# Gate and up of a feed-forward block: four of eight chunk pairs by seven products instead of three

## What is computed

```
y = _rms(h, norm_ffn_g[i])
h = h + (jax.nn.silu(y @ w_gate[i]) * (y @ w_up[i])) @ w_down[i]
```

## Time and profile before

| | |
|---|---|
| median of 3 runs | 1391.5 us (1391.1 to 1393.21) |
| the profiled execution: its time / its span | 1391.67 / 1389.9 us |
| PE busy | 1383.6 us (100%), 6233 matmuls |
| DVE busy | 1123.0 us (81%) |
| ACT busy | 822.8 us (59%) |
| POOL busy | 109.6 us (8%) |
| HBM read and written | 295.14 and 26.26 MB |
| clock granted to PE | full (2.4 GHz) in all 40 slices |

### The profile page before, as it was taken

How to read it: one execution, slowest core, us unless ns; L and a number is a source line. 1 busy time by engine, 2 the same in 40 slices (tenths; PEclk the granted TensorE clock), 3 DMA queues, 4 the chain that set the end, 5 groups by cost and what they waited for, 6 DMA issues and landing times.

```text
span 1389.9 us, 16815 instructions
## 1 busy us (share of the span) xinstructions
PE 1383.6 (100%) x6233; PEld 1133.3 (82%) x6233; DVE 1123.0 (81%) x1338; ACT 822.8 (59%) x1111; POOL 109.6 (8%) x96
## 2 busy tenths in 40 slices
...
GB/s 333 247 209 211 200 178 230 285 242 227 277 260 264 210 172 269 258 274 232 280 241 198 257 227 240 275 307 244 277 245 289 209 265 260 256 269 299 191 204 151
DMA packets 178538, 339.30 MB, mean 244 GB/s; under 512 B 12593, under 2 KB 36397, under 8 KB 178328
## 3 DMA queue, kind: packets, MB, share of 16 engines
q1 hardware_dynamic: 158968, 289.56, 64.0%
q0 software_dynamic: 6400, 23.49, 7.7%
...
HBM read 295.14 MB, written 26.26 MB: 231 GB/s over the span
## 4 chain that ended last, share of the span: by engine, by line
PE 92%; DMA 3%; DVE 3%; SPq 1%; ACT 1%; issue 0%; ACTq 0%; DVEq 0%
PE acc L2174 14%; PE acc L2177 14%; PE acc L2176 14%; PE acc L1996 14%; PE acc L1997 13%; PE acc L1998 13%; PE sp L2174 1%; PE sp L2177 1%; PE sp L2176 1%; PE tp L2177 1%; PE tp L2174 1%; PE tp L2176 1%; DVE w_lo L1278 1%; DMA w_raw<-in_w_in 1%; PE sp L2285 1%; DMA parked<-tile 1%
## 5 line engine op out<-in xcount | busy, mean ns | idle before, releaser
L868 ACT ACTIVATE w_hi<-w_raw 128x1024 fp32r<-128x1024 f32 x479 | 500.4, 1057 | 367.3 <-PE acc L1998 208.8
L1278 DVE TENSOR_TENSOR w_lo<-w_raw,w_hi 128x1024 fp32r<-128x1024 f32 x468 | 567.1, 1226 | 170.1 <-ACT w_hi L868 164.6
L1996 PE MATMUL acc<-w_lo,hh 128*128 128x512 f32 x528 | 207.9, 394 | 0.0
L1998 PE MATMUL acc<-w_hi,hl 128*128 128x512 f32 x528 | 205.6, 389 | 0.0
L1997 PE MATMUL acc<-w_hi,hh 128*128 128x512 f32 x528 | 205.6, 389 | 0.0
L2174 PE MATMUL acc<-w_lo,yh 128*128 128x512 f32 x512 | 199.3, 389 | 0.6 <-DVE w_lo L1278 0.6
L2177 PE MATMUL acc<-w_hi,yl 128*128 128x512 f32 x512 | 199.2, 389 | 0.0
L2176 PE MATMUL acc<-w_hi,yh 128*128 128x512 f32 x512 | 199.2, 389 | 0.0
L1996 PE MATMUL acc<-w_lo,yh 128*128 128x512 f32 x352 | 137.6, 391 | 0.3 <-DVE w_lo L1278 0.3
L1997 PE MATMUL acc<-w_hi,yh 128*128 128x512 f32 x352 | 137.0, 389 | 0.0
L1998 PE MATMUL acc<-w_hi,yl 128*128 128x512 f32 x352 | 137.0, 389 | 0.0
...
## 6 DMA issues: line engine op xcount, KB each, us to landing
...
```

The source lines that it names most:

```text
L868: act.activation(w_hi[:, v % SPL], src, ACT.Copy).then_inc(hi_ready, 1)
L1278: dve.tensor_tensor(w_lo[:, v % SPL], src, w_hi[:, v % SPL].bitcast(F32), ALU.subtract).then_inc(lo_ready, 1)
L1996: pe.matmul(dst, xh[:, f, tk], w_lo[:, v % SPL, k], start=(f == 0), stop=False)
L1998: last = pe.matmul(dst, xl[:, f, tk], w_hi[:, v % SPL, k], start=False, stop=(f == CK * n - 1))
```

## The change

`PAIR_PLAN` gets a fourth quad in place of a plain chunk pair (chunk 3) and a new order: 4 quads and 8 plain chunks, 24 splits. The first two quads' "g" now stand at the head of the pair, and the last four splits are the plain up chunks 7, 4, 5, 6. `TRIPLES` goes from 3 to 4, so that the sums of activations take 16 KB per partition, and the places of all other work in the pair are given anew. In the first pair one up chunk moves behind the gate's last two. To make room, `h_wide` now lies over the last quarter of `hh` for its first two uses and in `tile[7]` for the third, `h_sums` to where `big` lies, and one scratch result of ACT's squares to `big`.

```
-PAIR_PLAN = plain(0, 4, 3) + quad("g", 0) + plain(1, 4) + quad("g", 1) + quad("g", 2) + quad("u", 0) + quad("t", 0)
-PAIR_PLAN += quad("s", 0) + plain(1, 5) + quad("u", 1) + plain(0, 6, 5) + quad("t", 1) + quad("s", 1) + quad("u", 2)
-PAIR_PLAN += quad("t", 2) + quad("s", 2) + plain(0, 7) + plain(1, 7, 3, 6)
+PAIR_PLAN = quad("g", 0) + quad("g", 1) + plain(0, 4, 6) + quad("u", 0) + quad("t", 0) + quad("s", 0)
+PAIR_PLAN += quad("g", 2) + quad("u", 1) + quad("t", 1) + quad("s", 1) + quad("g", 3) + quad("u", 2)
+PAIR_PLAN += quad("u", 3) + plain(0, 7, 5) + quad("t", 2) + quad("s", 2) + quad("t", 3) + quad("s", 3)
+PAIR_PLAN += plain(1, 7, 4, 5, 6)
-SUMS = dict(copied={1: [0], 5: [1], 10: [2]}, summed={0: 5, 1: 11, 2: 14})
+SUMS = dict(copied={0: [0], 2: [1], 9: [2], 12: [3]}, summed={0: 3, 1: 5, 2: 14, 3: 16})
-FIRST_PLAN += quad("s", 1) + plain(1, 5) + plain(0, 6, 7) + plain(1, 6, 7)
+FIRST_PLAN += quad("s", 1) + plain(0, 6, 7) + plain(1, 5, 6, 7)
-           1: dict(hidden=1, turn=2, m1=12, mix=19, gate=20, low=21, silu=21, put=9, fetch=12, **SUMS),
-           2: dict(hidden=1, sums=4, turn=5, m1=12, mix=19, gate=20, low=21, silu=21, put=10, fetch=13, **SUMS),
+           1: dict(hidden=2, turn=11, low=22, put=12, fetch=13, m1=17, mix=21, gate=21, silu=23, **SUMS),
+           2: dict(sums=4, hidden=2, turn=11, low=22, put=12, fetch=13, m1=17, mix=21, gate=21, silu=23, **SUMS),
...
-TRIPLES, PAIRS_OF_DOWN = 3, 2
+TRIPLES, PAIRS_OF_DOWN = 4, 2
...
+        with ExitStack() as first:
+            first.enter_context(nc.sbuf_tensor("hh_front", [P, 12, S], F32))
+            h_wide_front = first.enter_context(nc.sbuf_tensor("h_wide", [P, PAIRS_OF_DOWN, 4, P], F32))
```

More of the change, by code:

```diff
@@ L120 @@
               + plain(1, 7, 4, 2) + plain(0, 6) + plain(1, 6, 3)]
-SUMS = dict(copied={1: [0], 5: [1], 10: [2]}, summed={0: 5, 1: 11, 2: 14})
 FIRST_PLAN = plain(0, 2) + plain(1, 2) + plain(0, 3) + plain(1, 3) + quad("g", 0) + quad("g", 1) + quad("u", 0)
 FIRST_PLAN += plain(0, 4) + quad("t", 0) + quad("s", 0) + plain(1, 4) + quad("u", 1) + plain(0, 5) + quad("t", 1)
-FIRST_PLAN += quad("s", 1) + plain(1, 5) + plain(0, 6, 7) + plain(1, 6, 7)
-FIRST_AT = dict(resid=1, turned=2, low2=3, request=3, low3=11, m1=13, mix=18, gate=19, silu=19,
+FIRST_PLAN += quad("s", 1) + plain(0, 6, 7) + plain(1, 5, 6, 7)
+FIRST_AT = dict(resid=1, turned=2, low2=3, request=3, low3=10, m1=13, mix=18, gate=19, silu=19,
                 copied={2: [0], 5: [1]}, summed={0: 6, 1: 11})
-PAIR_AT = {0: dict(add=1, m1=12, mix=19, gate=20, silu=21, **SUMS),
-           1: dict(hidden=1, turn=2, m1=12, mix=19, gate=20, low=21, silu=21, put=9, fetch=12, **SUMS),
-           2: dict(hidden=1, sums=4, turn=5, m1=12, mix=19, gate=20, low=21, silu=21, put=10, fetch=13, **SUMS),
-           3: dict(hidden=1, turn=2, m1=12, sums_high=17, mix=19, gate=20, sums_low=21, low=21, silu=21, put=9, fetch=12,
+SUMS = dict(copied={0: [0], 2: [1], 9: [2], 12: [3]}, summed={0: 3, 1: 5, 2: 14, 3: 16})
+PAIR_AT = {0: dict(add=1, m1=17, mix=21, gate=21, silu=23, **SUMS),
+           1: dict(hidden=2, turn=11, low=22, put=12, fetch=13, m1=17, mix=21, gate=21, silu=23, **SUMS),
+           2: dict(sums=4, hidden=2, turn=11, low=22, put=12, fetch=13, m1=17, mix=21, gate=21, silu=23, **SUMS),
+           3: dict(sums_high=14, sums_low=16, hidden=2, turn=11, low=22, put=12, fetch=13, m1=17, mix=21, gate=21, silu=23,
                    **SUMS)}
@@ L324, in build @@
                                     for n in ("y_sums_hi", "y_sums_lo"))
+        tile += [sb(f"tile{i}", [P, 1024]) for i in range(4, 8)]
+        with ExitStack() as first:
             h_sums_hi, h_sums_lo = (first.enter_context(nc.sbuf_tensor(n, [P, PAIRS_OF_DOWN, 4, P], F32R))
                                     for n in ("h_sums_hi", "h_sums_lo"))
-            h_wide = first.enter_context(nc.sbuf_tensor("h_wide", [P, PAIRS_OF_DOWN, 4, P], F32))
-        tile += [sb(f"tile{i}", [P, 1024]) for i in range(4, 8)]
         big = sb("big", [P, D])
@@ L526, in build, with h_wide @@
         ]
+        def h_wide(r):
+            return h_wide_front[:] if r < 2 else tile[7][:].rearrange("p (c f n) -> p c f n", c=PAIRS_OF_DOWN, f=4)
         def turn_buffers(n):
@@ L956, in square @@
             def square(row, j, junk=6):
+                into = big[:, 0:1024].rearrange("p (t n) -> p t n", t=T) if junk is big else tok(junk)
                 if row or j:
@@ L960, in square @@
                 for t in range(T):
-                    act.activation(tok(junk)[:, t], resid[:, t, CW * j:CW * (j + 1)], ACT.Square,
+                    act.activation(into[:, t], resid[:, t, CW * j:CW * (j + 1)], ACT.Square,
                                    accum_out=ssq[:, row, t, j:j + 1]).then_inc(squares, 1)
@@ L1081, in h_sums_to_high @@
                 act.wait_ge(h_sums, 4 * r + 4)
-                act.activation(h_sums_hi[:], h_wide[:], ACT.Copy).then_inc(h_sums_high, 1)
+                act.activation(h_sums_hi[:], h_wide(r), ACT.Copy).then_inc(h_sums_high, 1)
             def pair(m):
@@ L1094, in pair @@
                         wait_left(act, OUT_UNIT + 3)
-                        square(1, 3, junk=7)
+                        square(1, 3, junk=big)
                     if i == b.at.get("low3"):
```

6 lines of the change are left out of this document (3 added, 3 removed).

## The result

The changed kernel takes 1404.1 us (median of 6 runs, 1402.7 to 1405.1) against 1391.8 us (6 runs, 1391.1 to 1393.2). The ratio on record is 1.0082, 95% interval 1.0072 to 1.0092; the two medians alone give 1.0089. It is 0.8 to 0.9% slower, where 1385.4 us and "faster" were forecast, and it lies outside the range. The rival that was given 0.13, "the fourth add comes late", named the sign and the place; its 1399.4 us is still 4.7 too low.

The account below looks back on a forecast made before the run. PE was taken as the bound, busy 1383.6 of 1389.9 us. -6.80 - 1.00 + 1.12 + 0.60 = -6.08 against the profiled 1391.67 gave 1385.6, and 1385.4 us at the runs' median; range 1383.0 to 1391.5.

Parts of the forecast that it names:

- the fourth add comes late: Rival: the fourth adding DMA shares engines with loads, lands at 24.9 us of the pair; stalls 16.4, 1399.4 us; chance 0.13.
- What goes: Pairs 1 to 10: each turns 24 matmuls into 21, so 30 matmuls go, saving 6.80 us.
- The end of pair 0: Seam to pair 1: the last gate chunk comes 2.72 us earlier, so pair 1's loss of 1.00 us is regained.
- The heads of pairs 2 and 6: Start of these pairs: DVE's four `h_wide` sums delay splits, 0.9 us each against 0.34 now, 1.12 us more in all.
- `sums_low` in pairs 3 and 7: This 1.14 us operation stands between the fourth add's landing and its split: 0.3 us lost each, 0.6 in all.
- The ring: Split slots' turn of 2.57 us against 2.72 at chunk 7: margin 0.15, loss taken as 0, bound 0.3 per pair.
- The tail: End of a pair: DVE's result work and next split take 5.3 us against two plain runs, 5.44; fits by 0.2.
- second rival: Small losses in all pairs: chunk 7's margin of 0.15 does not hold, 3.0 us in all, 1388.4 us; chance 0.15.
- The fourth add: New adding DMA per pair, issued near 15.5 us: takes 6.7 us, lands at 22.2, nothing lost in ordinary pairs.
- The limit for its landing, 24.0: Fourth adding DMA: landing up to 24.0 us into the pair loses nothing, as "s2" is wanted at 25.84.

Follow-up runs that it names:

- e3: The kernel before with only the first pair's order changed (one up chunk behind the last two gate chunks, low half one place earlier); 1391.4 us against 1392.6, ratio 0.9989.
- e18: The changed kernel with every adding DMA of pairs 1 to 10 moving only 16 of 1024 columns; 1390.2 us against 1392.5 for the kernel before, ratio 0.9982.
- e1: The changed kernel with the adding DMA of every fourth quad moving only 16 of 1024 columns; 1393.3 us against 1392.6 for the kernel before, ratio 1.0006.

## Why the prediction was wrong, step by step

- **What goes, 6.80 us:** right. PE has 6203 matmuls, and a pair takes 40.80 us and its stall.
- **The end of pair 0, 1.00:** right in size (e3: 42.48 to 41.48), but in the kernel before two thirds come back in pair 2; in the changed one pair 1 has its own losses (2.2, and 0.7 in e18).
- **The heads of pairs 2 and 6, 0.9 each:** right. e18 has 0.98 each beyond an ordinary pair.
- **`sums_low` in pairs 3 and 7, 0.3 each:** 0.5 each with adds for nothing.
- **The ring, "I take 0":** it is 0.12 per pair. In pair 5 of e18 chunk 7's split was ready 0.08 us ahead of PE and not 0.15, and PE's next matmul came 0.10 late. ACT had its slot in time; DVE came to the split 0.07 later than in pairs 4 and 8, which have no transposition of a result in front of it and lose 0.06. **The tail, "it fits by 0.2":** 0.22 per pair. The split was ready after 5.5 us, not 5.3 (the last of the three `mix` operations holds DVE for 1.32 us, not 1.14). Both terms left out what PE loses on the matmuls behind a wait, 0.13 to 0.15 us behind a clear one. Together they are 0.33 in eight pairs and 0.28 in pairs 4 and 8, 3.2 us, close to the 3.0 of the second rival, which came true beside the first one. With 0.35 more in pair 1 and the terms above, e18's 6.5 us stand against 2.4 in the forecast: a miss of 4.1.
- **The fourth add, "I take 6.7, nothing lost":** this step failed. The add took 7.6 to 9.9 us to land, and its size cost 10.3 us (e1); the other three adds, which had no term, cost 4.1 more, 14.4 in all. The limit for its landing, 24.0, was right; the landing time was not. The median of 31 adds mixed three places. In the kernel before the second adds took 4.5 to 6.5 us, the third ones, the only ones at this place of the pair, 6.5 to 8.8 (7.1 in pair 5), but for 5.1 and 4.5 in pairs 4 and 8, which have no store and fetch. The fourth is issued 4.5 us behind the third, while it and two loads (chunk 5 of gate, chunk 7 of up) are still moving, and the store and chunk 4's load follow within 1.3 us.
- **The rival's own working:** landing at 24.9 was foreseen, 23.3 to 26.3 came, with "t3" late by 0.34 to 0.38 in nine of the ten pairs, as it said. It gave 1.54 us to each of eight pairs and nothing to 4 and 8, though these had 1.8 and 1.0. It took the share of the engines in pair 5 to rise from 0.90 to 0.97; it is 0.89, and the rows above have 0.84 to 0.91. The add is late long before the share reaches one. And the other three adds were not in it (4.1), nor the second rival.
- **The chances:** with the share at 0.90, a margin of 1.8 us over a median with a spread of 4.3 (4.5 to 8.8) was given 0.13 to fail. That was too little by the rows themselves. The top of that spread, 15.5 + 8.8 = 24.3, was already past the point, before one more add was put in.

2.4 + 4.1 + 14.4 is 20.9; 1385.4 + 4.1 + 14.4 = 1403.9, against 1404.1 measured.
